# Block scaling by 1/rms moved from GpSimd to VectorE in six of seven sections

## The chip, the cores and the metric

The kernel runs on one core of one Trainium2 chip. The metric is the device time of one execution in microseconds; before the change its median is 3639.61 us over three runs (3635.76 to 3640.41).

## The reference

The input x is 256 tokens by 2048 channels, fp32. Three transformer blocks follow one another. The first mixes an RWKV-7 recurrence with a chunked band attention, the second a top-k sparse attention with a spatial gating unit (SGU), the third a pooling mixer with a dilated attention; the second and third end in a feed-forward of width 8192. Each projection starts from an RMS norm:

```
h    = x * rsqrt(mean(x*x) + 1e-6) * g
proj = h @ w_in                      # then split into q, k, v, gates, ...
```

For the second block, which most of the change touches:

```
h = rms_norm(x, norm1_g)
q, k, v, qi, ki, wi, u_s, v_s, ga, gb = split(h @ w_in)
attn   = sparse_attention(q, k, v, qi, ki, wi, rel_bias)        # 16 heads, 4 kv heads, 256 tokens
sgu    = gelu(u_s) * (w_s @ layer_norm(gelu(v_s)) + b_s)        # per group of 128 channels, causal
merged = sigmoid(ga) * attn + sigmoid(gb) * sgu
x      = x + merged @ w_out
```

The factor 1/rms belongs to a token, so the kernel multiplies x by the gain g only, runs the projection, and scales the finished sums by 1/rms (the tile rstd, 128 x 256). This scaling of sums is what the change moves.

## The kernel before

All weight products go through one list of sections (the list `order`), in this order: qkv, za, rkv, gates, zr, branch, out for the first block; index2, qkv2, v2, u2, ga2, gb2, out2, up2_0, down2_0, up2_1, down2_1 for the second; in3, out3p, out3a, up3_0, down3_0, up3_1, down3_1 for the third. A section has blocks of 256 output channels, and a block has slots of four 128-row chunks of weights (four slots in all sections that matter here). There are 1084 slots and 255 blocks.

For each slot ScalarE copies the weights to a high part (L2205, `split_high`), VectorE subtracts it from the weights to make the low part (L2212, `split_low`), and TensorE multiplies: eight matmuls of 512 columns with the high part (L2282) and eight of 256 columns with the low part (L2288). Three slots of parts are buffered. SyncE loads a unit of two slots into a ring of four (L2195) once the low split of the unit that was there is done.

At the end of a block ScalarE copies one half of the PSUM sums to SBUF (L1845), VectorE adds the other half to it (L1932), and then the 128 x 512 result is multiplied by 1/rms. The functions `sums_scalar`, `sums_vector` and `sums_pool` write these steps. For a section named in `on_pool` (L227) GpSimd multiplies (L1895); for the others VectorE does (L1936), in phase 1. ScalarE and, for sections with activations, VectorE follow in later phases. The phase in which ScalarE waits for the scaling (`wait_scaled`, L235) is 3 for sections in `on_pool` and 1 for the others, and it waits there for every scaled section, also where it has nothing to compute on the block. The activations of gates, ga2 and gb2 (tanh, L1858 for the latter two) stand in that same phase, and VectorE's gating operations (L1981 for ga2; L1987 and L1989 for gb2) in phase 3 or 2.

The order of everything is written out by hand. Each engine walks over the places q = 0, 1, 2, ... (one place is one slot). When block b has ended at place q, ScalarE's order is: phase 0 (the copy), side work due at q, the high split of slot q+2, phase 1, side work due at q+0.34, phase 2, then phase 3 of a block that ended at q-1, side work due at q+0.67. VectorE's order is: phase 0 (the add), side work at q, the low split of slot q+2, phase 1, side work at q+0.34, phase 2, side work at q+0.67, and phase 3 of a block that ended at q-1. At the last block of a section phases 1 to 3 run at once, ahead of the side work and the split. All engines work through their instructions in this order, so a wait holds everything behind it.

Side work comes from threads, each with a start place and a pace. Those that run beside the six sections are: the low-rank projections of RWKV (beside qkv); the selection of the top-k keys (`select`, beside qkv2: L1351 and L1354 on VectorE); two attention threads of the second block (from v2 to u2: L1187 and L1181 stage operands, L1387 to L1390 add masks to logits, L1222 and L1223 are exponentials on ScalarE, L1197 to L1202 normalise on VectorE, L1249 transposes on TensorE, L1226 copies on ScalarE, L1253 to L1255 multiply by v on TensorE); `gelu_v` (L1420) and `gelu_u` (L1427) at the fourth and eighth blocks of v2 and u2; the statistics of the SGU beside ga2 (L1478 centres, L1469 squares on ScalarE, L1453 sums on TensorE); and two gating threads from ga2 to gb2 (L1528 copies on ScalarE, L1516 masks the transposed weights on VectorE, L1549 and L1550 mix on TensorE, L1522 multiplies by u on VectorE).

Of the kernel before, what the change touches and what calls it, by code (L numbers as in the profile page):

```python
# [117 lines left out]
def build_kernel(nc, I, out_dram):  # L118
    ctx = ExitStack()
    with ctx:  # L120
# [3 lines left out]
        def sem(name):  # L124
            return ctx.enter_context(nc.semaphore(name))
# [98 lines left out]

            return S[name].slot0 + (b + 1) * S[name].slots

        on_pool = ("qkv", "gates", "qkv2", "v2", "u2", "ga2", "gb2")  # L227
        scaled_by, scaled0, n_scaled = {}, {}, {True: 0, False: 0}
        for s in order:
            if s.name not in ("branch", "out", "out2", "down2_0", "down2_1", "down3_0", "down3_1"):  # L230
# [8 lines left out]
        def over(tile, n):  # L239

            return tile[:, 0:TOK].rearrange("p (o t) -> p o t", o=1).to_broadcast([P, n, TOK])
# [175 lines left out]
        def start_vector(v):  # L417
# [32 lines left out]
        n_summed, n_meaned, n_rooted, n_spread, n_copied = (  # L450
            sem(x) for x in ("n_summed", "n_meaned", "n_rooted", "n_spread", "n_copied"))
# [1436 lines left out]
        def sums_pool(pool, s, b):  # L1888
            if s.name in on_pool:
                if b == 0:  # L1890
                    pool.wait_ge(n_copied, norm1.copied if s.name[-1] == "2" else 1)
                k = s.block0 + b
                to = copies[s.name](b) if s.name in copies else stage[:, k % 2]
                pool.wait_ge(block_evacuated, k + 1)
                pool.tensor_tensor(to, to, over(rstd, 2), ALU.mult).then_inc(scaled_by_pool, 1)  # L1895
            if s.name == "out":
                post.add(pool, b)
            elif s.name in next_norm:
                next_norm[s.name][0].add(pool, b)
            elif s.name == "down3_1":  # L1900
                final3.add(pool, b)
# [153 lines left out]
        norm1 = Rms("norm1", 4, 4, high, 0, [rstd], own=True)  # L2055
# [130 lines left out]
        for u in range(n_slots // 2):  # L2186
            s, b, n = where[2 * u]
# [38 lines left out]
        with nc.Block() as block:  # L2226
# [18 lines left out]
            @block.gpsimd  # L2245
            def _(pool):
                side = Beside(pool, "gpsimd", threads)
                side.run(-1)
                for q in range(n_slots + 1):
                    if ended(q):  # L2250
                        sums_pool(pool, *ended(q))
                    side.run(q)
                    side.run(q + 0.34)
                    side.run(q + 0.67)
                side.run(n_slots + 9)
# [99 lines left out]
```

## Time and profile before

| | |
|---|---|
| median of three runs | 3639.61 us |
| profiled execution, its own time | 3641.87 us |
| its span in the trace | 3640.1 us |
| TensorE matmul busy | 3492.9 us (96%) |
| VectorE busy | 2225.8 us (61%) |
| ScalarE busy | 1581.7 us (43%) |
| GpSimd busy | 276.9 us (8%) |

The span is from the first to the last instruction that the profiler saw; the execution's own time is 1.8 us longer. Busy shares are of the span. TensorE's share is near full over the whole span, and the other engines' shares say little by themselves: they matter where TensorE waits for one of them.

### The profile page before, as it was taken

How to read it: one execution, taken by the hardware profiler on the slowest of the kernel's cores; microseconds unless marked ns; L12 is line 12 of the kernel's file. 1: busy time of each engine (PE TensorE's matmuls, PEld its weight loads, DVE VectorE, ACT ScalarE, POOL GpSimd, SP SyncE). 2: the span in 40 equal slices, each digit the busy share in tenths (PEclk: the TensorE clock that was granted, in tenths of full speed). 3: DMA queues.
4: the chain of work that ended last, by engine and by line, in shares of the span. 5: the costliest groups of instructions: out<-in, count | busy, mean ns of one | idle time of the engine just before them, and what ended most of it. 6: DMA issues, size and time to landing. Idle time of an engine off the chain costs nothing.

```text
span 3640.1 us, 53150 instructions
## 1 busy us (share of the span) xinstructions
PE 3492.9 (96%) x22326; PEld 3009.5 (83%) x22326; DVE 2225.8 (61%) x3130; ACT 1581.7 (43%) x2140; POOL 276.9 (8%) x313
## 2 busy tenths in 40 slices
PE   7999999988998999999999999999999899999998
PEld 6887777767886887887888888888888788888887
DVE  5556654555746667665676546655677766456644
ACT  3444333333453445443544434444454444434444
POOL 2100122220010110000000000001000000000000
PEclk9999999989998999999999999999999999999999
DMA  6554332323653554544566556665545466566653
GB/s 187 172 176 146 116 119 91 97 90 106 219 180 88 185 174 151 174 139 139 185 183 188 185 186 184 189 193 185 175 151 161 150 187 191 188 186 186 187 183 127
DMA packets 587351, 591.44 MB, mean 162 GB/s; under 512 B 20886, under 2 KB 581350, under 8 KB 587111
## 3 DMA queue, kind: packets, MB, share of 16 engines
q1 hardware_dynamic: 587112, 588.04, 51.9%
q8 instruction: 176, 2.88, 0.3%
q14 instruction: 63, 0.52, 0.0%
HBM read 581.68 MB, written 6.32 MB: 162 GB/s over the span
## 4 chain that ended last, share of the span: by engine, by line
PE 86%; DVE 8%; ACT 3%; issue 2%; DMA 1%; SPq 0%; POOL 0%; ACTq 0%; DVEq 0%
PE gp L2282 50%; PE gp L2288 27%; PE sidep L1026 4%; DVE w_parts L2212 2%; ACT w_parts L2205 1%; PE sidep L516 1%; ACT lo_half L1845 0%; PE sidep L1549 0%; PE sidep L1550 0%; DMA high<-bias_rows 0%; DVE stage L1932 0%; DVE stage L1936 0%; DVE smalls L94 0%; DVE smalls L92 0%; PE sidep L1320 0%
## 5 line engine op out<-in xcount | busy, mean ns | idle before, releaser
L2212 DVE TENSOR_TENSOR w_parts<-ring,w_parts 128x1024 fp32r<-128x1024 f32 x1084 | 1375.0, 1277 | 917.5 <-ACT w_parts L2205 916.4
L2205 ACT ACTIVATE w_parts<-ring 128x1024 fp32r<-128x1024 f32 x1084 | 1134.2, 1056 | 1100.0 <-PE gp L2288 1040.9
L2282 PE MATMUL gp<-x_parts,w_parts 128*128 128x512 f32 x5856 | 1534.7, 402 | 28.4 <-issue 12.7
L2282 PEld LDWEIGHTS gp<-x_parts,w_parts 128*128 128x128 f32 x5856 | 1065.2, 192 | 230.9 <-issue 30.8
L2288 PEld LDWEIGHTS gp<-x_parts,w_parts 128*128 128x128 f32 x5856 | 802.3, 192 | 63.5 <-DVE w_parts L2212 5.7
L2288 PE MATMUL gp<-x_parts,w_parts 128*128 128x256 f32 x5856 | 837.5, 286 | 3.7 <-DVE w_parts L2212 3.7
L2282 PE MATMUL gp<-ff_parts,w_parts 128*128 128x512 f32 x2816 | 715.9, 396 | 4.8 <-ACT w_parts L2205 4.8
L2282 PEld LDWEIGHTS gp<-ff_parts,w_parts 128*128 128x128 f32 x2816 | 505.1, 188 | 101.8 <-ACT w_parts L2205 5.6
L2288 PEld LDWEIGHTS gp<-ff_parts,w_parts 128*128 128x128 f32 x2816 | 385.3, 188 | 32.0
L2288 PE MATMUL gp<-ff_parts,w_parts 128*128 128x256 f32 x2816 | 394.9, 282 | 0.0
L1845 ACT ACTIVATE lo_half<-gp 128x512 f32<-128x512 f32 x255 | 152.2, 597 | 479.6 <-PE gp L2288 479.4
L1932 DVE TENSOR_TENSOR stage<-gp,lo_half 128x512 f32<-128x512 f32 x184 | 127.1, 691 | 208.7 <-ACT lo_half L1845 208.6
L504 POOL TENSOR_TENSOR low<-low 128x512 f32<-128x512 f32 (+1 forms) x44 | 65.0, 1483 | 1971.6 <-ACT low L492 1319.3
L1861 ACT ACTIVATE ff_parts<-stage 128x512 fp32r<-128x512 f32 x64 | 40.5, 633 | 170.5 <-DVE stage L1967 170.5
L1026 PEld LDWEIGHTS sidep<-high 64*64 64x64 f32 x1760 | 68.4, 136 | 45.0 <-issue 18.8
L1026 PE MATMUL sidep<-high 64*64 64x64 f32 (+1 forms) x1760 | 81.9, 230 | 17.7 <-ACT high L1008 5.3
L1895 POOL TENSOR_TENSOR high<-high,rstd 128x512 f32<-128x512 f32 x40 | 56.3, 1408 | 517.0 <-DVE high L1932 517.0
L1932 DVE TENSOR_TENSOR high<-gp,lo_half 128x512 f32<-128x512 f32 x63 | 43.5, 691 | 62.2 <-ACT lo_half L1845 62.2
L1895 POOL TENSOR_TENSOR stage<-stage,rstd 128x512 f32<-128x512 f32 x32 | 43.7, 1365 | 411.3 <-DVE stage L1932 411.3
L1992 DVE TENSOR_TENSOR ff_parts<-stage,ff_parts 128x512 fp32r<-128x512 f32 x64 | 44.3, 692 | 49.1 <-ACT ff_parts L1861 49.1
L1936 DVE TENSOR_TENSOR stage<-stage,rstd 128x512 f32<-128x512 f32 x88 | 60.3, 685 | 0.2
L1967 DVE SCALAR_TENSOR_TENSOR stage<-stage 128x512 f32<-128x512 f32 x64 | 44.3, 692 | 2.2
(372 smaller groups left out, 1751.9 us busy)
## 6 DMA issues: line engine op xcount, KB each, us to landing
ring<-w_in SPq DMA_DIRECT2D x220, 1024.0 KB, 5.2
ring<-w_ff SPq DMA_DIRECT2D x128, 1024.0 KB, 5.6
ring<-w_up SPq DMA_DIRECT2D x64, 1024.0 KB, 5.8
ring<-w_down SPq DMA_DIRECT2D x64, 1024.0 KB, 5.5
ring<-w_out SPq DMA_DIRECT2D x48, 1024.0 KB, 5.5
ring<-w_branch_rwkv SPq DMA_DIRECT2D x8, 1024.0 KB, 5.5
ring<-w_branch_attn SPq DMA_DIRECT2D x8, 1024.0 KB, 5.4
gate_scratch<-stage SPq DMA_DIRECT2D x16, 256.0 KB, 2.3
```

Of the source, the lines that this page charges most:

```text
L504: m = pool.tensor_tensor(self.acc[k], self.acc[k], self.sq[b - 1][k], ALU.add)
L1026: return pe.matmul(out, lhs, rhs, start=start, stop=stop, skip_group_check=True)
L1845: act.activation(lo_half[:, k % 2], gp[:, k % 2, :, 1, :], ACT.Copy).then_inc(lo_copied, 1)
L1895: pool.tensor_tensor(to, to, over(rstd, 2), ALU.mult).then_inc(scaled_by_pool, 1)
L1932: v.tensor_tensor(to, gp[:, k % 2, :, 0, :], lo_half[:, k % 2], ALU.add).then_inc(block_evacuated, 1)
L1936: v.tensor_tensor(to, to, over(scaled_by[s.name], 2), ALU.mult).then_inc(scaled_by_vector, 1)
L1967: v.scalar_tensor_tensor(st, st, 0.0, st, ALU.max, ALU.mult).then_inc(finished_up, 1)
L1992: v.tensor_tensor(ff_parts[:, 2 * b:2 * b + 2, 1, :], st, ff_parts[:, 2 * b:2 * b + 2, 0, :].bitcast(F32), ALU.subtract).then_inc(ff_split, 1)
L2205: act.activation(w_parts[:, q % PARTS, 0], ring[:, u % RING, SLOT * (q % 2):SLOT * (q % 2) + SLOT, :], ACT.Copy).then_inc(high_split, 1)
L2212: v.tensor_tensor(w_parts[:, q % PARTS, 1], ring[:, u % RING, SLOT * (q % 2):SLOT * (q % 2) + SLOT, :], w_parts[:, q % PARTS, 0].bitcast(F ...
L2282: pe.matmul(gp[:, k % 2, j, :, :], w_parts[:, q % PARTS, 0, c, j * P:(j + 1) * P], operand(s, b, SLOT * n + c), start=(n == 0 and c == 0), ...
L2288: m = pe.matmul(gp[:, k % 2, j, 0, :], w_parts[:, q % PARTS, 1, c, j * P:(j + 1) * P], operand(s, b, SLOT * n + c)[:, 0, :], start=False, ...
```

## The change

The list of sections whose sums GpSimd scales shrinks from seven to one. In qkv, qkv2, v2, u2, ga2 and gb2 (12, 12, 8, 8, 8 and 8 blocks, 56 in all) VectorE now multiplies; in gates (16 blocks) GpSimd still does. As the phases are chosen by that list, ScalarE's wait for the scaling and its tanh move from phase 3 to phase 1 in these sections, and VectorE's gating operations of ga2 and gb2 from phase 3 to phase 2. GpSimd's wait at the start of a section loses the case for the second block.

```diff
-        on_pool = ("qkv", "gates", "qkv2", "v2", "u2", "ga2", "gb2")
+        on_pool = ("gates",)
...
         def sums_pool(pool, s, b):
             if s.name in on_pool:
                 if b == 0:
-                    pool.wait_ge(n_copied, norm1.copied if s.name[-1] == "2" else 1)
+                    pool.wait_ge(n_copied, 1)
```

## Rows read from the trace of the kernel before

**Rows 1.** The page, part 1: busy time, share, instructions of TensorE.
```profile
PE 3492.9 (96%) x22326; PEld 3009.5 (83%) x22326; DVE 2225.8 (61%) x3130; ACT 1581.7 (43%) x2140; POOL 276.9 (8%) x313
```
**Rows 2.** The page, part 4: the chain that ended last, shares by engine.
```profile
PE 86%; DVE 8%; ACT 3%; issue 2%; DMA 1%; SPq 0%; POOL 0%; ACTq 0%; DVEq 0%
```
**Rows 3.** Busy times by windows, the sum over the six sections, us.
```profile
sum 770.90, PE 745.98 PEld 640.46 DVE 481.62 ACT 326.62 POOL 78.21; mean PE 124.33 PEld 106.74 DVE 80.27 ACT 54.44 POOL 13.03
```
**Rows 4.** The instructions of L1895: count, duration min/median/max ns, first and last start.
```profile
L1895 POOL TENSOR_TENSOR high<-high,rstd x40: 1265/1292/3237, 46.1 to 1526.0; 128x512 f32<-128x512 f32 x40
```
**Rows 5.** Timeline, VectorE, qkv2: start, duration, instruction, idle before and its releaser.
```profile
1293.81 2.19 DVE L2212 TENSOR_TENSOR w_parts<-ring,w_parts 128x1024 fp32r<-128x1024 f32 x1 [0.26 <-ACT w_parts L2205]
```
**Rows 6.** Timeline, VectorE and ScalarE, a block end of in3.
```profile
2592.16 1.23 DVE L2212 TENSOR_TENSOR w_parts<-ring,w_parts 128x1024 fp32r<-128x1024 f32 x1 [0.26 <-ACT w_parts L2205]
2593.30 0.68 DVE L1936 TENSOR_TENSOR high<-high,rstd 128x512 f32<-128x512 f32 x1
...
2594.02 1.06 ACT L2205 ACTIVATE w_parts<-ring 128x1024 fp32r<-128x1024 f32 x1 [1.89 <-DVE high L1936]
```
**Rows 7.** Timeline, TensorE, qkv2 after the top-k selection.
```profile
1201.58 1.22 PE L2288 MATMUL gp<-x_parts,w_parts 128*128 128x256 f32 x8 [1.08 <-DVE w_parts L2212]
```
**Rows 8.** Who waited for L1936, the largest: us in all, times.
```profile
  ACT w_parts L2205: 48.0, 23
```
**Rows 9.** Timeline, three engines, the fourth block end of v2.
```profile
1362.72 1.28 ACT L1420 ACT_TABLE_LOAD   x1
...
1363.04 1.22 DVE L1390 TENSOR_TENSOR low<-low 128x384 f32<-128x384 f32 x1
...
1364.83 1.21 DVE L2212 TENSOR_TENSOR w_parts<-ring,w_parts 128x1024 fp32r<-128x1024 f32 x1
...
1368.54 0.17 DVE L1197 COPY smalls<-smalls 128x2 f32<-128x2 f32 x1 [0.73 <-ACT low L1223]
...
1369.55 0.55 PE L1249 MATMUL sidep<-ident,low 128*128 128x128 f32 x3 [1.25 <-DVE low L1202]
```
**Rows 10.** Timeline, VectorE and TensorE, the fourth block end of u2.
```profile
1479.11 2.19 DVE L2212 TENSOR_TENSOR w_parts<-ring,w_parts 128x1024 fp32r<-128x1024 f32 x1 [0.26 <-ACT w_parts L2205]
...
1485.74 0.38 PE L1253 MATMUL sidep<-low 128*128 128x128 f32 x2
```
**Rows 11.** Timeline, VectorE and TensorE, the second block end of ga2.
```profile
1559.91 2.32 DVE L2212 TENSOR_TENSOR w_parts<-ring,w_parts 128x1024 fp32r<-128x1024 f32 x1
...
1561.89 1.84 PE L1453 MATMUL sidep<-ones,low 128*128 128x1 f32 x16
```
**Rows 12.** Timeline, ScalarE and TensorE, from the end of ga2 into gb2.
```profile
1648.00 0.63 ACT L1858 ACTIVATE stage<-stage 128x512 f32<-128x512 f32 x1 [2.13 <-POOL stage L1895]
...
1651.36 0.48 PE L1549 MATMUL sidep<-high,ones 1*128 1x128 f32 x2 [3.33 <-DVE low L1516]
```
**Rows 13.** Timeline, VectorE and TensorE, the first three block ends of gb2.
```profile
1668.74 2.00 DVE L2212 TENSOR_TENSOR w_parts<-ring,w_parts 128x1024 fp32r<-128x1024 f32 x1 [0.53 <-ACT w_parts L2205]
1670.65 0.48 DVE L1516 TENSOR_TENSOR low<-sidep,consts 128x128 f32<-128x128 f32 x2
...
1670.99 0.48 PE L1549 MATMUL sidep<-high,ones 1*128 1x128 f32 x2 [1.35 <-DVE low L1516]
...
1673.10 0.68 DVE L1987 SCALAR_TENSOR_TENSOR stage<-stage,high 128x512 f32<-128x512 f32 x1
...
1687.17 0.48 PE L1549 MATMUL sidep<-high,ones 1*128 1x128 f32 x2
...
1699.99 2.20 DVE L2212 TENSOR_TENSOR w_parts<-ring,w_parts 128x1024 fp32r<-128x1024 f32 x1 [0.26 <-ACT w_parts L2205]
...
1703.28 0.48 PE L1549 MATMUL sidep<-high,ones 1*128 1x128 f32 x2
```
**Rows 14.** Busy times by windows behind the stall of 1651.36; PEclk is the granted clock.
```profile
1652.00:1656.00 4.00, 4.00 (x15) 2.52 (x14) 1.81 (x4) 0.00 (x0) 0.00 (x0) 0.65 0.54 163
1656.00:1660.00 4.00, 4.00 (x14) 3.39 (x14) 0.42 (x1) 0.00 (x0) 0.00 (x0) 0.50 0.30 103
```

## The prediction, made before the change was run

> **What bounds the kernel now.** I read the page's busy shares first and then the chain. TensorE is busy 3492.9 us, 96% of the span, and 86% of the chain that ended last is its own work [rows 1, 2]. So a change on other engines counts only where it moves a matmul. Next came the busy times by windows of the six sections that the diff touches (qkv, qkv2, v2, u2, ga2, gb2): of 770.9 us TensorE is busy in 746.0 [rows 3]. Only 25 us of idle stand there, which is all that the change could ever give back directly; what it could cost is not limited so. Then the 56 places where the change acts, the ends of 56 weight blocks, in the timelines of ScalarE, VectorE, GpSimd and TensorE.
>
> **What a block end looks like.** At a block end ScalarE copies the low half out of PSUM, VectorE adds (0.69 us), GpSimd multiplies by 1/rms in 1.29 us (median) [rows 4]. Meanwhile VectorE starts the low split of slot q+2, and this takes 2.19 us where GpSimd's multiply lies beside it [rows 5], against 1.23 us alone [rows 6]. GpSimd's multiply therefore already costs VectorE about 0.96 us. The Trainium skill (SBUF — State Buffer, Who interferes with whom) says that a VectorE instruction with two SBUF inputs and a GpSimd operation that reads SBUF exclude each other for a whole instruction; by that rule the multiply is not hidden on GpSimd now, and removing it is a gain that I weigh as a rival below.
>
> **Part 1, VectorE's time.** Removed are 56 multiplies of 1.29 us on GpSimd with some 0.7 us of lock on average: in the six sections VectorE's instructions beside a GpSimd multiply are longer than alone by 38 us in all (the excess of 2.19 over 1.23 at about 40 blocks; at the others GpSimd waited, or the neighbours had one SBUF input). Added are 56 x 0.68 us = 38 us of multiply on VectorE. The two cancel. VectorE at about 62% busy (481.62 of 770.90 [rows 3]) has room, so this alone is worth nothing either way, except in one stretch: during the top-k of qkv2 VectorE runs without a gap from 1183 to 1201 us (its operations there have one SBUF input and are not held up), and TensorE waits 1.08 us for the low split at its end [rows 7]. One multiply falls in it: +0.7 us.
>
> **Part 2, ScalarE now waits early.** This is the part that decides. For a section that GpSimd scales, ScalarE waits for the multiply in phase 3, a slot later, when it is long done. For the others it waits in phase 1, straight after its high split, and VectorE's multiply comes only after its low split, which itself waits for that high split. The in3 section, which VectorE scales already, shows the price: low split starts at 2592.16, multiply at 2593.30, and ScalarE stands idle 1.89 us until 2594.02 [rows 6]. So "ready" is low split start + 1.86 us. ScalarE waited 48.0 us in 23 such places in the trace [rows 8]. Where no side thread runs this is hidden: the high split of slot q+3 begins 0.7 us late and is needed some 3 us later. But everything that ScalarE has to do at q+0.34 (exponentials, gelu, squares, transposes' copies) now stands behind that wait, and side threads' matmuls stand in TensorE's own queue. Of the 56 ends these move a matmul:
>
> v2, fourth block. The low split starts at 1364.83 behind a masked add stretched by the lock to 1.22 us [rows 9] from 0.56 (the same operation at 1366.61); without the lock it starts at 1364.17, so the scaling is ready at 1366.03. Now the activation table for gelu is loaded at 1362.72, ahead of the wait [rows 9]. With a wait in phase 1 ahead of it, the load (1.28 us) starts only at 1366.05 and gelu at 1367.33, 3.3 us later than now (1362.72 + 1.28 = 1364.0). The queue behind it (four gelus, a table load, the exponentials) has no gaps, so VectorE's copy at 1368.54, which waits for an exponential, moves by 3.3 us and so does TensorE's transpose at 1369.55, which already waits 1.25 us [rows 9]. +3.3 us; if the load still goes ahead of the waits, +2.0.
>
> u2, fourth block. Ready at 1479.11 + 1.86 = 1480.97 [rows 10], where an exponential now starts at 1478.97, right behind the high split: 2.0 us later. Exponentials, a table load and four gelus follow without gaps, then the high split and the copy that attention's last matmul at 1485.74 needs. That copy would end at 1486.8: +1.1 us.
>
> ga2, second block. Low split at 1559.91 + 1.86 = 1561.77, then tanh (0.6), which now comes ahead of the square, then the square (1.06): done 1563.45, and the sum of squares stands at 1561.89 [rows 11]. +1.6 us.
>
> gb2, blocks 1 to 3. Here phase 3 of VectorE becomes phase 2 as well: it waits for tanh (0.63 us [rows 12]), does its two gating operations (0.68 and 0.69), and only then comes to the masked transpose (L1516) at q+0.67, where now these two come after it, at 1673.10 [rows 13]. Block 1: ready 1670.60, tanh to 1671.2, two operations to 1672.65, where L1516 started at 1670.65: +2.0 us on a matmul that already waits 1.35 us [rows 13]. Block 2 has the same shape, with its matmul at 1687.17 directly behind L1516: +2.0. Block 3: ready 1701.85, L1516 done at 1704.2, matmul at 1703.28 now: +0.9 [rows 13].
>
> **Part 3, section ends.** At a section's last block all phases run at once, and both ScalarE and the next split wait for the multiply. By GpSimd that is 2.09 us from the add's start (1645.91) to tanh at 1648.00, with 2.13 us of ScalarE idle [rows 12]; by VectorE it is two operations of 0.69 and 0.68 with their hand-overs, 1.45. That saves 0.64 us where TensorE hangs on it, at three of the six ends (v2's start over a bias table's DMA, u2's start, gb2's start at 1651.36 [rows 12]): -1.9 us. Eight smaller effects of 0.15 to 0.55 us of both signs (a shorter lock in qkv's fourth block, a later logits operand in u2's second, a late table DMA in v2's sixth) sum to about 0; I allow 1.5 us to either side.
>
> **The sum.** 0.7 + 3.3 + 1.1 + 1.6 + 4.9 - 1.9 = +9.7 us. To this comes the clock. After gb2's stall of 3.33 us the granted clock was 0.65 for 4 us and 0.50 for 4 us [rows 14], 1.2 of 2.4 GHz: (0.35 + 0.5) x 4 = 3.4 us lost. The stall of v2's fourth block grows from 1.25 to 4.5 us, longer than that one; gb2's first falls from 3.3 to 2.7 and its second rises from 1.35 to 3.4. I take one such stretch more than now: +3.4. Together +13.1 us on the profiled execution's 3641.87 us (span 3640.1 and 1.8 around it) gives 3655. That execution is 2.3 us above the median of the runs shown, 3639.61, so the forecast for the median is 3652.
>
> **Rivals.**
> (a) The lock is the cost, and its end the gain. TensorE's chain runs through held-up low splits at five places in v2, u2 and gb2, of 0.5 to 1.0 us each, 3.9 us in all; with 1.9 at the section ends and the slow clock of rows 14 gone (3.4) this gives -9 and 3630 us. It decides if ScalarE's and VectorE's later side work still meets its matmuls. For it: rows 5. Against it: behind the same split comes the new multiply (0.68), so the side work after it starts only 0.2 us earlier, or, with tanh, later. This is faster by 0.25%. 10%.
> (b) Everything stays under TensorE: the delays are real but thread steps have slack that I count too small, the table load goes ahead, no further slow stretch. Sum 9.7 - 1.3 = 8.4, and some 3 us of the gb2 terms gone: +5, 3645 us. For it: 41 of 56 ends move nothing at all. 26%.
> (c) A late stall feeds on itself: two more slow-clock stretches (v2 and gb2) and the small effects all against: 9.7 + 6.8 + 1.5 = +18, 3658 us. 14%.
> (d) Forecast, +9 to +15 us. 50%.
>
> **How the numbers follow.** A measurement of this kernel can tell about 0.2%, 7.3 us, from no change, so slower means above 3646.9. Slower: all of (c) and (d), and a tenth of (b) and its like: 0.66. Within 0.2%: the rest of (b) and the weak half of (a): 0.24. Faster: 0.10. The range that leaves out most of (a) and the end of (c) is 3637 to 3662; the forecast's own is 3648 to 3656.
>
> **What would show it.** In the changed profile GpSimd loses some 72 us of busy time and VectorE's total stays within 5 us; low splits at block ends of the six sections take 1.23 us. ScalarE shows waits on VectorE's L1936 that grow from 48 us by 50 us or more. TensorE shows a stall of about 4.5 us before a transpose (L1249) near 1372 us, stalls of 2 to 3.5 us before L1549 in gb2 at two places, and one new slow-clock stretch near 1375 us. All sections after out2 keep their length. I am wrong if the stall at v2's fourth block stays near 1.3 us, or if L1516 still starts before the gating operations in gb2.

## The result, and the profile after

The changed kernel takes 3670.52 us (median of 4 runs, 3665.31 to 3673.02) where the kernel before takes 3637.69 (4 runs, 3635.52 to 3640.41): a ratio of 1.0084, with a 95% interval of 1.0071 to 1.0096. The two medians are 33 us apart, the ratio gives 31. The forecast was 3652, with a range that ended at 3662: the sign was right and the size was not. The profiled execution of after took 3673.02 us, and its span is 3671.3.

The page of after, part 1, answers to [rows 1]:

```profile
PE 3513.8 (96%) x22326; PEld 3025.8 (82%) x22326; DVE 2222.3 (61%) x3186; ACT 1581.4 (43%) x2140; POOL 198.4 (5%) x257
```

TensorE runs the same 22326 matmuls and is busy 20.9 us longer. Its idle time (span less busy) goes from 147.2 to 157.5 us, +10.3. These two make the 31.2 us between the spans. VectorE took over 56 multiplies (38 us) and is still busy 3.5 us less: its 1084 low splits (L2212) took 1338.1 us in all and no longer 1375.0. GpSimd lost 78.5 us.

Busy times by windows, after: v2, u2, ga2 and gb2, and the sum over the six sections, which answers to [rows 3]. The columns are the window, its length, busy time (and instructions) of TensorE's matmuls and weight loads, VectorE, ScalarE and GpSimd, then the granted clock, the DMA share and GB/s:

```profile
...
1305.50:1426.50 121.00, 110.74 (x639) 97.02 (x638) 80.47 (x164) 56.88 (x99) 0.00 (x0) 0.96 0.51 157
1426.50:1533.20 106.70, 102.38 (x605) 89.26 (x604) 68.84 (x116) 54.45 (x83) 0.00 (x0) 1.00 0.51 158
1533.20:1657.80 124.60, 122.90 (x708) 105.33 (x707) 72.99 (x110) 50.55 (x65) 0.00 (x0) 0.99 0.47 145
1657.80:1788.00 130.20, 121.02 (x595) 100.94 (x595) 71.77 (x94) 46.40 (x58) 0.00 (x0) 0.86 0.41 127
sum 798.40, PE 764.17 PEld 654.37 DVE 476.39 ACT 326.24 POOL 2.96; mean PE 127.36 PEld 109.06 DVE 79.40 ACT 54.37 POOL 0.49
```

The same view of before, for v2 and gb2:

```profile
1304.00:1418.80 114.80, 106.83 (x639) 93.15 (x638) 80.39 (x156) 56.95 (x99) 12.14 (x8) 1.00 0.54 165
...
1645.90:1758.60 112.70, 108.00 (x596) 91.24 (x595) 72.55 (x87) 46.72 (x58) 10.36 (x8) 0.97 0.48 149
```

The six sections grew by 27.5 us (770.9 to 798.4). TensorE's idle time in them went from 24.9 to 34.2, +9.3; its busy time grew by 18.2 us on the same work. Of these 27.5 us, 17.5 stand in gb2, 6.2 in v2 and 3.9 in ga2. In gb2 the granted clock is 0.86 against 0.97. One less the clock, times the length, is what a window lost to it at most (where TensorE was idle, a low clock cost nothing): 0.14 x 130.2 = 18.2 us after and 0.03 x 112.7 = 3.4 us before. TensorE's busy time in gb2 grew by 13.0 us.

The stalls, TensorE's timeline of after: v2's fourth block [rows 9], u2's fourth [rows 10], ga2's second [rows 11], gb2's start [rows 12], and gb2's blocks 1 to 3 [rows 13]. The bracket holds the idle time before the matmul and what ended it:

```profile
1374.51 0.90 PE L1249 MATMUL sidep<-ident,low 128*128 128x128 f32 x3 [4.58 <-DVE low L1202]
...
1493.68 0.49 PE L1253 MATMUL sidep<-low 128*128 128x128 f32 x2 [1.18 <-ACT low L1226]
...
1571.92 1.28 PE L1453 MATMUL sidep<-ones,low 128*128 128x1 f32 x10 [1.34 <-ACT low L1469]
...
1662.58 0.48 PE L1549 MATMUL sidep<-high,ones 1*128 1x128 f32 x2 [2.69 <-DVE low L1516]
...
1685.80 0.79 PE L1549 MATMUL sidep<-high,ones 1*128 1x128 f32 x2 [3.40 <-DVE low L1516]
...
1709.54 0.48 PE L1549 MATMUL sidep<-high,ones 1*128 1x128 f32 x2 [2.14 <-DVE low L1516]
...
1729.67 0.48 PE L1549 MATMUL sidep<-high,ones 1*128 1x128 f32 x2 [0.95 <-DVE low L1516]
```

One of them in full: VectorE and ScalarE in gb2's first block after [rows 13]. The low split takes 1.23 us, no longer 2.00. Behind it stand the multiply, 0.80 us of waiting for tanh, and two gating operations, and only then L1516, for which TensorE waits:

```profile
1681.50 1.23 DVE L2212 TENSOR_TENSOR w_parts<-ring,w_parts 128x1024 fp32r<-128x1024 f32 x1 [0.53 <-ACT w_parts L2205]
...
1682.64 0.68 DVE L1936 TENSOR_TENSOR stage<-stage,rstd 128x512 f32<-128x512 f32 x1
1683.36 0.63 ACT L1858 ACTIVATE stage<-stage 128x512 f32<-128x512 f32 x1 [1.89 <-DVE stage L1936]
...
1684.13 0.69 DVE L1987 SCALAR_TENSOR_TENSOR stage<-stage,high 128x512 f32<-128x512 f32 x1 [0.80 <-ACT stage L1858]
...
1684.85 0.69 DVE L1989 TENSOR_TENSOR high<-high,stage 128x512 f32<-128x512 f32 x1
1685.46 0.48 DVE L1516 TENSOR_TENSOR low<-sidep,consts 128x128 f32<-128x128 f32 x2
```

And the clock, windows of 8 us of after through gb2 (same columns; [rows 14] showed one slow stretch in before):

```profile
1654.00:1662.00 8.00, 5.89 (x35) 4.95 (x33) 4.25 (x6) 4.45 (x7) 0.00 (x0) 1.00 0.42 132
1662.00:1670.00 8.00, 7.42 (x23) 5.35 (x24) 3.45 (x8) 0.01 (x1) 0.00 (x0) 0.62 0.43 131
1670.00:1678.00 8.00, 8.00 (x38) 6.90 (x37) 2.64 (x4) 2.12 (x2) 0.00 (x0) 0.74 0.01 2
1678.00:1686.00 8.00, 4.60 (x30) 3.97 (x29) 4.92 (x9) 3.67 (x6) 0.00 (x0) 0.90 0.43 131
1686.00:1694.00 8.00, 8.00 (x22) 5.63 (x23) 1.93 (x3) 0.00 (x0) 0.00 (x0) 0.50 0.43 131
1694.00:1702.00 8.00, 8.00 (x36) 6.90 (x35) 3.31 (x6) 2.12 (x2) 0.00 (x0) 0.75 0.00 0
...
1710.00:1718.00 8.00, 8.00 (x30) 6.14 (x30) 1.25 (x2) 0.77 (x1) 0.00 (x0) 0.61 0.41 131
...
1734.00:1742.00 8.00, 8.00 (x32) 6.67 (x33) 2.21 (x3) 1.06 (x1) 0.00 (x0) 0.69 0.18 61
```

After each of the four stalls the clock is down: 0.62 and 0.74, 0.50 and 0.75, 0.61, 0.69. In the window from 1686 TensorE is busy all 8 us and gets 22 matmuls done, at a granted clock of 0.50, which is 1.2 of 2.4 GHz. So the theory to test: the change costs by its early waits, not by the engine that multiplies; and most of the price is the clock behind short stalls, not the stalls.

### The profile page after: what moved, and what is told of

It is laid out like the page before. It is cut to its first block, busy times and chain, and to the rows that moved or that the text cites. A ratio compares the mean times of both kernels' runs of the same rounds, so it can differ in the third digit from the quotient of the medians.

```text
span 3671.3 us, 53200 instructions
## 1 busy us (share of the span) xinstructions
PE 3513.8 (96%) x22326; PEld 3025.8 (82%) x22326; DVE 2222.3 (61%) x3186; ACT 1581.4 (43%) x2140; POOL 198.4 (5%) x257
## 4 chain that ended last, share of the span: by engine, by line
PE 85%; DVE 8%; ACT 3%; issue 2%; DMA 1%; SPq 0%; POOL 0%; ACTq 0%; DVEq 0%
PE gp L2282 50%; PE gp L2288 26%; PE sidep L1026 4%; DVE w_parts L2212 2%; ACT w_parts L2205 1%; PE sidep L516 1%; PE sidep L1550 0%; PE sidep L1549 0%; DVE stage L1936 0%; ACT lo_half L1845 0%; DMA high<-bias_rows 0%; DVE stage L1932 0%; DVE smalls L94 0%; DVE smalls L92 0%; PE sidep L1320 0%
## 5 line engine op out<-in xcount | busy, mean ns | idle before, releaser
L2212 DVE TENSOR_TENSOR w_parts<-ring,w_parts 128x1024 fp32r<-128x1024 f32 x1084 | 1338.1, 1243 | 929.4 <-ACT w_parts L2205 928.5
L2288 PEld LDWEIGHTS gp<-x_parts,w_parts 128*128 128x128 f32 x5856 | 807.3, 194 | 64.6 <-DVE w_parts L2212 6.2
L1936 DVE TENSOR_TENSOR stage<-stage,rstd 128x512 f32<-128x512 f32 x104 | 71.2, 685 | 0.3
L1936 DVE TENSOR_TENSOR high<-high,rstd 128x512 f32<-128x512 f32 x63 | 43.2, 685 | 0.3
L1026 PE MATMUL sidep<-consts,high 64*64 64x64 f32 (+1 forms) x352 | 26.0, 256 | 14.9 <-DVE high L915 14.9
```

The lines of the kernel that those rows point to most:

```text
L1026: return pe.matmul(out, lhs, rhs, start=start, stop=stop, skip_group_check=True)
L1936: v.tensor_tensor(to, to, over(scaled_by[s.name], 2), ALU.mult).then_inc(scaled_by_vector, 1)
L2212: v.tensor_tensor(w_parts[:, q % PARTS, 1], ring[:, u % RING, SLOT * (q % 2):SLOT * (q % 2) + SLOT, :], w_parts[:, q % PARTS, 0].bitcast(F ...
L2288: m = pe.matmul(gp[:, k % 2, j, 0, :], w_parts[:, q % PARTS, 1, c, j * P:(j + 1) * P], operand(s, b, SLOT * n + c)[:, 0, :], start=False, ...
```

## The experiments

Each ran beside the kernel before on one chip, and its ratio is to those runs. Where an edit adds lines, the line numbers in its rows are higher by as many.

**All phases late, VectorE multiplies.** The rival was that the engine costs: a fuller VectorE.

```diff
+        scalar_late = ("qkv", "gates", "qkv2", "v2", "u2", "ga2", "gb2")
+        vector_late = ("qkv", "gates", "qkv2", "v2", "u2", "ga2", "gb2")
...
-            if s.name in scaled_by and phase == (3 if s.name in on_pool else 1):
+            if s.name in scaled_by and phase == (3 if s.name in scalar_late else 1):
...
-            elif phase == (3 if s.name in on_pool else 2):
+            elif phase == (3 if s.name in vector_late else 2):
```

> VectorE multiplies in all six sections as in the changed kernel, but ScalarE's wait and tanh and VectorE's gating stay in phase 3, as before the change. Theory W (the early waits are what costs, through stalls and the slow clock behind them): the stalls before the transpose in v2's fourth block (4.6 us) and before L1549 in gb2 (3.4, 2.1, 1.0) shrink to 1.3 or less, the slow clock of gb2 goes back to one stretch of about 7 us, and the time is 3632 to 3642 us, at or a little below the kernel before. Rival V (38 us of extra multiplies on VectorE cost by themselves, as VectorE holds up side threads): the time stays above 3655.

Measured: 3640.43 us (11 runs) against 3640.47, a ratio of 1.0001 (0.9987 to 1.0014). In total the engine alone costs nothing that can be told. Two of its rows, TensorE's fourth block of v2 and the window of gb2:

```profile
1373.36 0.90 PE L1251 MATMUL sidep<-ident,low 128*128 128x128 f32 x3 [3.25 <-DVE low L1204]
```

```profile
1650.70:1764.20 113.50, 109.47 (x596) 92.36 (x595) 71.63 (x94) 46.73 (x58) 0.00 (x0) 0.95 0.47 148
```

gb2 is back at 113.5 us. In v2 a stall of 3.25 us stays. ScalarE's timeline of this kernel says why:

```profile
1364.53 1.28 ACT L1422 ACT_TABLE_LOAD   x1
1367.82 2.19 ACT L1422 ACTIVATE high<-high 128x512 f32<-128x512 f32 x4 [2.01 <-DVE high L1938]
```

Here the table load goes ahead, and gelu itself waits 2.01 us for the sums that it reads, which VectorE scales later than GpSimd did. This is the prediction's other bound for this place (+2.0). v2 takes 118.2 us here against 114.8 before, so the engine does cost something in this one place; what makes up for it elsewhere was not traced. In after the load stands behind ScalarE's wait, and the stall is 4.58 us:

```profile
1367.69 1.28 ACT L1420 ACT_TABLE_LOAD   x1 [3.36 <-DVE high L1936]
```

**Early phases, GpSimd multiplies.** The mirror: the same three conditions in before, with only gates in both lists.

```diff
+        scalar_late = ("gates",)
+        vector_late = ("gates",)
```

> The opposite half: GpSimd multiplies in all seven sections as before the change, but ScalarE's wait and tanh come in phase 1 and VectorE's gating in phase 2 in the six. Theory W: it is slower than the kernel before by 5 to 20 us though VectorE does no multiply, as ScalarE's wait is shorter (GpSimd is ready about 1 us earlier than VectorE would be): gb2's second stall about 2.8 us, v2's fourth block about 2.3. Rival V: no difference from the kernel before, 3638.

Measured: 3653.63 us (4 runs), a ratio of 1.0041 (1.0028 to 1.0055). Not one multiply moved to VectorE, and the kernel is slower by 13 us between the medians, 15 by the ratio. Its window of gb2:

```profile
1647.90:1771.30 123.40, 115.63 (x596) 96.75 (x595) 72.44 (x87) 46.73 (x58) 10.35 (x8) 0.90 0.44 136
```

gb2 is 10.7 us longer than in before, and v2, whose fourth block stalls 2.45 us, is 5.5 us longer. Its stalls in gb2 are 3.33, 2.67 and 1.34 us, and the clock costs at most 0.10 x 123.4 = 12.3 us. Early waits alone give a slower kernel. With VectorE in the early phases they are longer (gb2's second stall is 3.40 us and not 2.67), as its multiply comes behind its split, and the loss is about twice as large. So neither half alone makes the 33 us.

**Which sections.** First gb2 alone on VectorE; then after, without ScalarE's wait where ScalarE has nothing to compute on the block.

```diff
-        on_pool = ("gates",)
+        on_pool = ("qkv", "gates", "qkv2", "v2", "u2", "ga2")
```

> VectorE multiplies in gb2 alone, with the early phases; GpSimd in the other six. If gb2's loss is its own (three stalls and their slow clock) it keeps about 130 us against 113 and the time is 3638 + 15 to 18 = 3653 to 3656. If the slow clock there needs the later start or ga2's changes ahead of it, the loss in gb2 is 5 to 10 us only.

```diff
-            if s.name in scaled_by and phase == (3 if s.name in on_pool else 1):
+            if s.name in scaled_by and s.name not in ("qkv", "qkv2", "v2", "u2") and phase == (3 if s.name in on_pool else 1):
```

> The changed kernel without ScalarE's wait in qkv, qkv2, v2 and u2, where ScalarE does nothing with the block in that phase. Theory W: v2 loses its 4.6 us stall (1.3 stays, or 2.5 as gelu itself waits for the scaling) and the slow clock behind it, u2 its 1.2 us: 6 to 9 us less than the changed kernel, 3662; ga2 and gb2 keep their lengths. Rival V: 0 to 1 us less.

Measured: gb2 alone 3654.05 (4 runs), 1.0037 (1.0023 to 1.0051), as expected. Without the idle waits 3657.31 (4 runs), 1.0045 (1.003 to 1.0061), some 5 us less than I had expected. The windows of gb2, first of the one, then of the other:

```profile
1637.10:1765.40 128.30, 118.48 (x595) 98.97 (x595) 71.06 (x93) 46.40 (x58) 1.29 (x1) 0.88 0.41 129
```

```profile
1645.70:1775.00 129.30, 120.11 (x596) 100.16 (x595) 71.80 (x94) 46.40 (x58) 0.00 (x0) 0.87 0.41 128
```

So gb2's eight blocks alone make 0.37 of the 0.84%, with four stalls as in after (3.40, 2.14 and 0.95 us; the first is 3.33 and not 2.69, as GpSimd still scales ga2). Without the idle waits v2 takes 116.1 us instead of 121.0, though its stall is still 3.24 us: with that wait gone, gelu waits for its data as in the first experiment.

**Which early wait in gb2.** ScalarE's phases stay early, and VectorE's gating of ga2 and gb2 goes back to phase 3 (conditions as in the first experiment).

```diff
+        scalar_late = ("gates",)
+        vector_late = ("gates", "ga2", "gb2")
```

> The changed kernel, but VectorE's gating operations of ga2 and gb2 stay in phase 3; ScalarE's wait and tanh stay in phase 1. If VectorE's order (it waits for tanh and gates before it masks the transposed weights) is what makes gb2's stalls, they go back to 2.7, 1.4, 0 and 0 us, gb2 to about 113 to 117 us and the time to 3655 to 3659; ga2 keeps its 1.3 us stall. Rival: ScalarE's wait makes them, as the copies of the gating threads stand behind it: the stalls stay above 2 us.

Measured: 3648.16 (8 runs), 1.0031 (1.0021 to 1.0041): 7 us below the lower end that I had expected. VectorE and TensorE in gb2's first block, and gb2's window:

```profile
1673.25 0.68 DVE L1938 TENSOR_TENSOR stage<-stage,rstd 128x512 f32<-128x512 f32 x1
...
1673.97 0.29 DVE L1518 TENSOR_TENSOR low<-sidep,consts 128x128 f32<-128x128 f32 x1
...
1674.31 0.48 PE L1551 MATMUL sidep<-high,ones 1*128 1x128 f32 x2 [1.31 <-DVE low L1518]
```

```profile
1648.40:1761.90 113.50, 109.45 (x596) 92.35 (x595) 71.41 (x94) 46.41 (x59) 0.00 (x0) 0.95 0.47 147
```

The masked transpose (here L1518) starts right behind the multiply and the stall is 1.31 us instead of 3.40, so gb2 has the 113.5 us of late phases. In gb2 it was VectorE's gating, with its wait for tanh, standing ahead of L1516, and not ScalarE's wait for the multiply. What is left over before (+11 us by the ratio) goes with v2, u2 and ga2, whose stalls of 4.58, 1.19 and 1.33 us stay; these three sections take 352.7 us, 10.8 more than in before.

**The clock by itself.** After, with 5, 7, 4 and 1 matmuls of no use ahead of the wait in gb2's four stalls. They write to columns that nobody reads then; the waits stay.

```diff
+                    if self.th == 0 and i >= 4:
+                        for _ in range((5, 7, 4, 1)[i - 4]):
+                            pe.matmul(self.y[:, 256:512], ident[:, :], vv[:, 0, :], start=True, stop=True, skip_group_check=True)
```

> The changed kernel with matmuls in the four stalls of TensorE at gb2's gating: ahead of the waits of the even thread's last four steps TensorE multiplies 5, 7, 4 and 1 times a 128x128 by a 128x256 into PSUM columns that nobody reads (0.43 us each at full clock by the pace of the statistics' matmuls: 2.1, 3.0, 1.7 and 0.4 us, each shorter than the stall of 2.7, 3.4, 2.1 and 1.0 us it stands in). The waits themselves stay. Theory C (idle stalls are what lowers the granted clock in gb2): slow clock in gb2 falls from 37 us to under 14 and the time by 10 to 15 us, to 3656 to 3661. Rival K (the clock falls for another reason, such as the mixing matmuls with one row, or the stalls act only by their own length): no change, 3671 within 3.

Measured: 3651.56 (4 runs), 1.0039 (1.0026 to 1.0053), against 1.0084 (1.0071 to 1.0096) without them. TensorE's timeline at gb2's start (each fp32 matmul leaves two records, so 5 are x10), and gb2's window:

```profile
1657.65 2.32 PE L1547 MATMUL sidep<-high,ident 128*128 128x256 f32 x10
1660.50 0.48 PE L1552 MATMUL sidep<-high,ones 1*128 1x128 f32 x2 [0.53 <-DVE low L1516]
```

```profile
1655.70:1769.90 114.20, 112.37 (x630) 95.18 (x629) 71.60 (x94) 46.39 (x58) 0.00 (x0) 1.00 0.46 145
```

This run separates the clock from the stall. Every useful matmul still waits as in after, but the clock stays at 2.4 GHz through all of gb2 (1.00 against 0.86), and gb2 takes 114.2 us instead of 130.2. These 16 us are what the clock cost there; the two medians differ by 19, the two ratios by 16.

All runs say the same, not only the profiled ones, as each has its span and mean granted clock (three digits, of which the last is worth 3.7 us in one run). Span times one less the clock, averaged over the runs, is 100.9 us in after, 84.0 here and 80.3 in the kernel before beside this one; the rest of the span is 3567.2, 3566.9 and 3556.3 us. The change therefore cost up to some 20 us of clock and 11 us of everything else, and the filling gave back 17 us of clock and nothing else. I had expected 3656 to 3661, having put too little on the clock even now.

**The same in v2.** The last one, and 20 products of 128 x 128 ahead of the wait at v2's fourth block.

```diff
+                        if self.name == "att2" and self.th == 0 and (i, r) == (0, 2):
+                            for _ in range(20):
+                                pe.matmul(y[:, 384:512], ident[:, :], ident[:, :], start=True, stop=True, skip_group_check=True)
```

> The filled kernel with a second filling: 20 products of two 128x128 tiles (0.21 us each, 4.3 us) ahead of TensorE's wait in v2's fourth block, where it stalls 4.6 us. The stalls' own length stays in the time, and only the clock should change. Theory C: v2's slow clock goes from 10 to 0 to 3 us and 4 to 5 us come back, so the time is 3645 to 3649, which is the kernel before plus the 9 us that the stalls themselves cost. Rival (v2's slow clock has another cause): 3651 to 3653.

Measured: 3649.29 (7 runs), 1.0031 (1.002 to 1.0042). TensorE's timeline there:

```profile
1370.22 4.63 PE L1247 MATMUL sidep<-ident 128*128 128x128 f32 x40
1374.98 0.55 PE L1252 MATMUL sidep<-ident,low 128*128 128x128 f32 x3
```

The time is just above the 3645 to 3649 expected. The stall is covered, but v2 still takes 120.3 us. The kernel to compare with is the last one, which has the same v2 without the filling. Its windows around the fourth block and 40 us later:

```profile
1368.00:1376.00 8.00, 4.84 (x22) 4.29 (x23) 4.03 (x10) 6.24 (x14) 0.00 (x0) 0.79 0.21 54
...
1408.00:1416.00 8.00, 7.75 (x39) 6.75 (x39) 6.18 (x14) 2.60 (x7) 0.00 (x0) 0.79 0.25 79
```

Here the granted clock is 1.00 from 1368 to 1384, so the slow stretch at the fourth block is gone, while the one from 1408 to 1416 is at 0.79 in both; after has 1.00 there. That second stretch therefore need not come from the filling: with the same instructions in v2 it came in one execution (the last kernel's) and not in another (after's). The intervals of this kernel and the last one overlap, so a gain from covering v2's stall is not shown.

**Multiplying right after the add.** With VectorE the multiply need not stand behind the split. Once with late phases (the three edits of the first experiment too), once with after's early ones.

```diff
-            late = 2 if s.name == "index2" and b == 0 else 1
+            late = 2 if s.name == "index2" and b == 0 else 0 if s.name in ("qkv", "qkv2", "v2", "u2", "ga2", "gb2") else 1
```

> VectorE multiplies in all six sections right after the add, ahead of the side work and the low split, with the late phases of the kernel before. The scaling is ready 1.45 us after the add's start, as early as GpSimd had it (1.37 after the add's end, 2.09 at section ends), so v2's fourth stall is 1.3 us and not 3.2, and the lock is gone. Theory W: 3630 to 3638, 1 to 8 us under the kernel before and under the late phases alone. Rival: the low split, 0.4 us later, stalls TensorE in qkv2's top-k: no gain, 3640.

> As the one before, but with the changed kernel's early phases. ScalarE's wait is then some 0.5 us and not 2 us. Theory W: v2's fourth block stalls 2.3 us, as with GpSimd in the early phases, and gb2's three stalls are about 0.7 us shorter than in the changed kernel, so the time is 3648 to 3658. If the loss were the early phases themselves whatever the length of the wait, it would stay at 3671.

Measured: with late phases 3638.06 (12 runs), 1.0005 (0.9994 to 1.0015), no change and not the gain that I had expected; with early ones 3644.27 (10 runs), 1.0014 (1.0004 to 1.0024), below the 3648 to 3658 expected. The window of gb2, late and then early:

```profile
1639.70:1751.10 111.40, 107.90 (x596) 91.24 (x595) 71.82 (x94) 46.73 (x59) 0.00 (x0) 0.97 0.48 151
```

```profile
1642.90:1765.70 122.80, 117.08 (x596) 98.03 (x595) 71.75 (x94) 47.03 (x58) 0.00 (x0) 0.89 0.44 137
```

With late phases v2's fourth block stalls 1.24 us and v2 takes 115.2 us, so the 3.25 us of the first experiment came from the multiply's place behind the split. With early ones, the order of two instructions on VectorE takes back most of what the change cost, with every phase as in after. ScalarE then waits 0.26 us for the multiply in gb2's first block instead of 1.89. But the two gating operations still stand ahead of the masked transpose, and a stall of 2.14 us is left at gb2's second mixing, and with it up to 0.11 x 122.8 = 13.5 us of clock.

**The best of both.** Multiply right after the add, late phases, and 5 and 1 idle matmuls in the two gb2 stalls that are left (2.69 and 0.81 us).

```diff
+                    if self.th == 0 and i in (4, 5):
+                        for _ in range((5, 1)[i - 4]):
+                            pe.matmul(self.y[:, 256:512], ident[:, :], vv[:, 0, :], start=True, stop=True, skip_group_check=True)
```

> Multiply right after the add on VectorE, late phases, and the filling (5 and 1 matmuls of 0.43 us) in the two stalls that gb2 still has there (2.7 and 0.8 us). Theory C: gb2's one slow stretch of 7 us goes, 3 us come back, 3633 to 3637, under the kernel before. Rival: what is gained is within the spread, 3638.

Measured: 3632.97 (11 runs) against 3637.29, a ratio of 0.9985 (0.9974 to 0.9996). Its window of gb2:

```profile
1644.70:1753.10 108.40, 107.49 (x608) 91.05 (x607) 71.85 (x94) 46.75 (x59) 0.00 (x0) 1.00 0.50 155
```

This beats both kernels, by 0.15% over before, with an interval that just leaves out 1; it is also the best of ten variants, so the gain is weakly shown. gb2 takes 108.4 us where before took 112.7, 4.3 us less, and the medians differ by as much. Over all runs, span times one less the clock is 71.7 us here, 79.7 with the new order alone and 81.5 in before, which points to the matmuls. How much of the gain they bring and how much the new order is not settled: the interval of this kernel (up to 0.9996) touches that of the one without them (from 0.9994).

## Why the prediction was wrong

- **What bounds the kernel: right.** 27.5 of the 31.2 us lie in the six sections, as TensorE's waits and the clock behind them. VectorE's total stayed (2225.8 to 2222.3), GpSimd lost 78.5 us (72 forecast), and up2_0 to down3_1 kept their lengths within 2 us.
- **Part 1: right, and small.** VectorE's time cancelled. The stall behind the top-k [rows 7] went from 1.08 to 1.40 us, +0.3 where I had +0.7. At gb2's first block the low split went from 2.00 to 1.23 us. The Trainium skill's lock (SBUF — State Buffer, Who interferes with whom) is what these rows look like. Its end did not make a faster kernel, as rival (a) needed it to: with all phases late, where it is gone too, the ratio was 1.0001.
- **Part 2: right in each place.** v2's fourth block 4.58 us (4.5 forecast: +3.3, with the table load behind the wait), u2's +1.18 (+1.1), ga2's +1.34 (+1.6), gb2's first block 3.40 (3.4), the second 2.14 (+2.0) and the third 0.95 (+0.9). ScalarE's waits for L1936 grew from 48.0 us [rows 8] to this, in the same view of after:

```profile
  ACT w_parts L2205: 106.4, 50
```

- **Part 3: right.** TensorE's stall at gb2's start went from 3.33 to 2.69 us, at u2's from 1.12 to 0.49 and at v2's from 3.29 to 2.79, together -1.8 where I had -1.9.
- **The sum of the stalls: right.** +9.7 forecast, +9.3 measured in the six sections. The places named above come to +9.5, so this is no luck of two errors. In the prediction's arithmetic two slips changed nothing: 3641.87 + 13.1 - 2.3 is 3652.7, not 3652, and the weak half of (a) was counted both as faster and as within 0.2%.
- **The clock: this is the step that failed.** "I take one such stretch more than now: +3.4." TensorE's busy time on the same matmuls grew by 20.9 us, 13.0 of them in gb2 and 3.9 in v2. The stretch that I named, behind v2's fourth block, is there at the size I gave it (granted clocks of 0.86 and 0.71 in two windows of 8 us from 1368, 3.4 us). Those in gb2 I did not have. I had reasoned that gb2's first stall shrinks from 3.33 to 2.69 and its second only takes its place, so no stretch is added; but the first, shrunk, kept its slow stretch, and 3.40, 2.14 and 0.95 us each drew another. With their 13.0 us in place, 9.7 + 3.4 + 13.0 is 26.1 of the 31.2 us between the spans; of the other 5.1 us, 4.5 are longer busy time in small pieces (2.7 of them outside the six sections, in3 alone being 1.6 us longer), most likely the clock too. Rival (c) had the right mechanism at a third of the price: it allowed two more stretches of 3.4 us, +6.8, where TensorE's busy time grew by 20.9.

The price could not have been read from one row: [rows 14] were one stall and what followed it. Two places in the trace of before show how far it can vary. TensorE's stall of 3.29 us in v2, in a window whose granted clock is 1.00 (above), cost no clock that the window shows:

```profile
1316.84 0.44 PE L1236 MATMUL sidep<-ident,low 128*128 128x128 f32 x2 [3.29 <-DVE low L1181]
```

In after the same stall was shorter, 2.79 us, and the window of 8 us from 1320, behind it, is at 0.84:

```profile
1317.81 0.44 PE L1236 MATMUL sidep<-ident,low 128*128 128x128 f32 x2 [2.79 <-DVE low L1181]
...
1320.00:1328.00 8.00, 8.00 (x41) 7.07 (x41) 6.31 (x16) 4.51 (x11) 0.00 (x0) 0.84 0.42 133
```

And index2, where TensorE waits 2.17, 2.42, 6.59 and 3.71 us within 22 us, ran at 0.76 of the clock, and lost at most 0.24 x 64.6 = 15.5 us:

```profile
1085.30:1149.90 64.60, 50.37 (x252) 44.35 (x252) 44.36 (x100) 26.00 (x38) 5.67 (x2) 0.76 0.32 83
```

gb2 after the change has four stalls in 67 us and lies nearer to the second. Had I taken index2's 15.5 us as the upper end for the clock, the sum would have reached 9.7 + 15.5 = +25 us, about 3665 us: outside the range that I gave, and still some 6 us short of the result. No row of before shows the whole price.

## What to carry to other kernels

When an operation moves to another engine, look at which phase or place the list that moves it also moves: here the engine alone cost nothing that can be told, the early waits alone about 15 us, and the two together about 33, because the waits became longer. Cost each new stall of TensorE twice, once for itself and once for the clock behind it, and where several small ones fall close together take the price from a stretch of the trace that already has such a group, not from a single one, and give it a wide range. An in-order engine should do first what others wait for; a multiply put ahead of a split instead of behind it took back most of the loss, with no wait removed.

## What the runs showed of the hardware

- Stalls of 0.95 to 3.4 us, four of them in 67 us, kept TensorE at a mean of 0.86 of its clock over 130 us; filled with matmuls of no use they left it at 1.00, and the section was 16 us shorter. The Trainium skill (TensorE: Matmul & The Clock Gate, A second HAM failure mode: psum-queue depth-cycling) tells of frequent short idles between groups of matmuls that let the clock swing; gb2 agrees, with up to 18.2 us lost. A stall of 3.29 us in v2 of before showed no loss, and the same stall at 2.79 us in after was followed by a window at 0.84, so the length of a stall does not decide by itself.
- Where in v2 the clock fell changed from one execution to the next: with the same v2, after has 1.00 from 1408 to 1416 and the kernel with gb2 filled has 0.79. What decides if a given short stall is followed by a slow stretch stays open.
- The spread of one kernel's times goes with the clock. In the kernel before, beside the last experiments, the run of 3655.27 us had a mean granted clock of 0.973 and the run of 3633.63 us one of 0.980.
- An activation table load (1.28 us) stood behind a wait placed ahead of it in the code, with ScalarE idle for 3.36 us; without a wait there it ran ahead, and only the activation waited (2.01 us).
- Single runs of the unchanged kernel lay between 3631.64 and 3655.66 us on the chips used for the experiments, so differences of some 5 us here rest on the intervals, not on single profiles.
